# A hybrid decoder trunk: in the forgetting layer, three of four groups of probabilities are turned by VectorE and carried through DRAM

## The reference

```python
h = rmsnorm(x, g[0]); y = mixer(h); x = x + rmsnorm(y, g[1])
h = rmsnorm(x, g[2]); y = (silu(h @ Wg) * (h @ Wu)) @ Wd; x = x + rmsnorm(y, g[3])
```

```python
q, k, v, f_logit = split(h @ w_in)            # 32 heads of 64
c = cumsum(log_sigmoid(f_logit + b_f))        # per head, over tokens
s = q k^T / 8 + c_q - c_k, causal
p = softmax(s); out = (p v) @ w_out
```

## Time and profile before

| what | value |
|---|---|
| median of 3 runs | 2127.06 us (2127.04 to 2127.35) |
| profiled execution, its own time | 2127.44 us |
| its span in the trace | 2125.5 us |
| PE busy | 2115.1 us (100%), 9795 instructions |
| DVE (VectorE) busy | 1587.3 us (75%) |
| ACT (ScalarE) busy | 1180.5 us (56%) |
| POOL busy | 121.0 us (6%) |
| HBM traffic | 188 GB/s over the span |

### The profile page before, as it was taken

The page is one execution under the profiler, slowest core; times in us unless marked ns, Lnnn a source line. Parts: engine busy times, 40 slices in busy tenths (PEclk is TensorE's granted clock), DMA queues, the critical chain, the costliest instruction groups (busy, mean ns, idle before and its releaser), DMA issues.

```text
span 2125.5 us, 32513 instructions
## 1 busy us (share of the span) xinstructions
PE 2115.1 (100%) x9795; PEld 1735.5 (82%) x9795; DVE 1587.3 (75%) x3257; ACT 1180.5 (56%) x2133; POOL 121.0 (6%) x231
## 2 busy tenths in 40 slices
PE   9999999999999999999999999999999999999998
PEld 7877888888888888888878877888888888888886
DVE  6777577877668876678787777577776778776786
ACT  7776565544555444555676566565454555445453
POOL 2111000000000000000231131000000000000000
PEclk9999999999999999999999999999999999999999
DMA  7544856555666655665665664666655665556652
GB/s 259 189 139 133 215 180 219 187 188 177 203 211 190 195 172 193 197 206 156 185 197 182 181 195 160 207 199 198 198 174 182 197 216 187 187 179 198 216 186 91
DMA packets 205692, 399.85 MB, mean 188 GB/s; under 512 B 13248, under 2 KB 13664, under 8 KB 205104
## 3 DMA queue, kind: packets, MB, share of 16 engines
q1 hardware_dynamic: 203008, 389.86, 58.6%
q0 software_dynamic: 2320, 8.72, 1.4%
q10 hardware_dynamic: 288, 0.33, 0.0%
HBM read 396.72 MB, written 2.13 MB: 188 GB/s over the span
## 4 chain that ended last, share of the span: by engine, by line
PE 98%; DVE 1%; issue 1%; DMA 0%; POOL 0%; ACT 0%; SPq 0%; POOLq 0%; DVEq 0%; ACTq 0%
PE bank L1233 31%; PE bank L1235 31%; PE bank L1234 31%; PE bank L1282 1%; PE bank L1309 1%; PE bank L1293 1%; PE bank L1246 1%; DMA x_sb<-x 0%; PE bank L1265 0%; DVE ring_lo L759 0%; DVE x_sb L802 0%; DVE y_sb L1027 0%; POOL post_r L1126 0%; DVE a_lo L766 0%; DVE y_sb L795 0%
## 5 line engine op out<-in xcount | busy, mean ns | idle before, releaser
L1233 PE MATMUL bank<-ring_hi,a_hi 128*128 128x512 f32 x2240 | 884.0, 395 | 0.6 <-DVE ring_lo L759 0.6
L1235 PE MATMUL bank<-ring_hi,a_lo 128*128 128x512 f32 x2240 | 873.2, 390 | 0.0
L1234 PE MATMUL bank<-ring_lo,a_hi 128*128 128x512 f32 x2240 | 872.1, 389 | 0.0
L557 ACT ACTIVATE ring_hi<-stage,g_t 128x512 fp32r<-128x512 f32 x992 | 663.2, 717 | 340.1 <-DMA stage<-ffn_w_gate_up 202.4
L759 DVE SCALAR_TENSOR_TENSOR ring_lo<-stage,g_t,ring_hi 128x512 fp32r<-128x512 f32 x992 | 708.8, 760 | 162.1 <-ACT ring_hi L557 160.1
L1235 PEld LDWEIGHTS bank<-ring_hi,a_lo 128*128 128x128 f32 x2240 | 420.4, 188 | 88.8
L1233 PEld LDWEIGHTS bank<-ring_hi,a_hi 128*128 128x128 f32 x2240 | 420.6, 188 | 88.2 <-issue 4.1
L1234 PEld LDWEIGHTS bank<-ring_lo,a_hi 128*128 128x128 f32 x2240 | 421.0, 188 | 83.4
L757 DVE TENSOR_TENSOR ring_lo<-stage,ring_hi 128x512 fp32r<-128x512 f32 x480 | 306.7, 690 | 131.5 <-ACT ring_hi L555 130.2
L555 ACT ACTIVATE ring_hi<-stage 128x512 fp32r<-128x512 f32 x480 | 277.3, 624 | 167.7 <-PE bank L1235 150.0
L1233 PE MATMUL bank<-ring_hi,h_hi 128*128 128x512 f32 x704 | 274.4, 390 | 0.0
(11 more groups left out here) (144 smaller groups left out, 855.8 us busy)
## 6 DMA issues: line engine op xcount, KB each, us to landing
stage<-ffn_w_gate_up SPq DMA_DIRECT2D x352, 512.0 KB, 4.6
stage<-ffn_w_down SPq DMA_DIRECT2D x176, 512.0 KB, 5.6
stage<-fox_w_in SPq DMA_DIRECT2D x96, 512.0 KB, 4.1
stage<-swa_w_in SPq DMA_DIRECT2D x48, 512.0 KB, 4.5
stage<-swa_w_out SPq DMA_DIRECT2D x64, 256.0 KB, 4.1
stage<-fox_w_out SPq DMA_DIRECT2D x32, 512.0 KB, 4.6
g_b<-norm_gains POOLq DMA_DIRECT2D x4, 1024.0 KB, 5.9
cum_b<-cum_scratch POOLq DMA_DIRECT2D x32, 128.0 KB, 3.4
```

The costliest lines, as they stand in the source:

```text
L557: nc.scalar.activation(ring_hi[:, n % RING, :], src, ACT.Identity, scale=g_t[:, row * KT + j:row * KT + j + 1]).then_inc(hi_ready, 1)
L1233: nc.tensor.matmul(dst, hi_a, hi_w, start=start, stop=False)
L1234: nc.tensor.matmul(dst, hi_a, lo_w, start=False, stop=False)
L1235: return nc.tensor.matmul(dst, lo_a, hi_w, start=False, stop=stop)
```

## The change

It touches only the forgetting layer. The order of its units becomes keys, queries, values. A group's attention starts in its own value unit and goes on through the next two units, by a new table `FOX`; the last group has the table `FOX_LAST`. In the first three groups, P is no longer transposed by PE and copied by ScalarE. After each `normalise` (a pair of heads), VectorE turns the pair in 32x32 blocks inside each set of 32 partitions into `p_blocks` (one buffer). ScalarE stores `p_blocks` to DRAM in one DMA and, later, loads the blocks to their partitions in four DMAs of 32 partitions each into `p_f` (two buffers). `times_v` reads P from `p_f` with runs of 32 columns, one pair of heads at a time. The last group is turned on PE as before. Keys are turned in the query unit. POOL's bias loop is written out, and its buffers come free with the turned P. The steps of the forget gate and of the output's first heads are moved.

```diff
+FOX = dict(scores={6: (0, 1), 26: (2, 3)},
+           maxima={6: (0, 1), 12: (2, 3), 26: (4, 5), 32: (6, 7)},
+           exps={7: 0, 8: 1, 13: 2, 14: 3, 27: 4, 28: 5, 33: 6, 34: 7},
+           scaled={11: 0, 17: 1, 31: 2, 37: 3}, turned={},
+           pv={41: (0,), 52: (1,), 61: (2,), 72: (3,)}, out={53: 0, 73: 1},
+           stored={18: 0, 29: 1, 38: 2, 49: 3}, loaded={28: 0, 38: 1, 48: 2, 59: 3})
+FOX_LAST = dict(scores={6: (0, 1), 26: (2, 3)},
+                maxima={6: (0, 1), 8: (2, 3), 26: (4, 5), 28: (6, 7)},
...
+                pv={35: (0, 1), 52: (2, 3)}, out={})
-FG_STEPS = dict(split=34, gate=42, copy=44, turn=46, z=48, exp=50, log=52, cumulate=56, read=57)
+FG_STEPS = dict(split=28, gate=36, copy=38, turn=40, z=42, exp=44, log=46, cumulate=50, read=51)
-KEYS_TURNED = {True: (26, 27, 28, 30), False: (3, 7, 11, 15)}
+KEYS_TURNED = (1, 4, 7, 10)
 QUERIES_TURNED = (18, 20)
+LATE_O_FOX = {0: [(0, 1)], 2: [(1, 1)], 4: [(2, 1)], 6: [(3, 1)], 8: [(4, 1)], 10: [(5, 0), (5, 1)],
+              14: [(6, 0), (6, 1)], 27: [(7, 0), (7, 1)]}
...
+        p_f = at("p_f", 38 * KB + 256, [P, 2, P // Q, 6, Q])
+        p_blocks = at("p_blocks", 12 * KB, [P, P // Q, 6 * Q])
...
-            if U_FOX + 3 <= u <= U_FOX_OUT and (u - U_FOX) % 3 == 0:
-                return NG + (u - U_FOX) // 3 - 1
+            if U_FOX <= u < U_FOX_OUT and (u - U_FOX) % 3 == 2:
+                return NG + (u - U_FOX) // 3
...
+            def store_probabilities(G, i, m):
+                act.wait_ge(p_turned, HP * (G - NG) + m + 1 + HP * i)
+                act.dma_start(p_dram[m], p_blocks[:, :, :].rearrange("p b r -> p (b r)")).then_inc(p_stored, 16)
+
+            def load_probabilities(G, i, m):
+                act.wait_ge(p_stored, 16 * (HP * (G - NG) + m + 1) + 16 * HP * i)
...
+                blocks = p_dram[m].rearrange("(a j) (b r) -> b j a r", a=P // Q, b=P // Q)
+                for b in range(P // Q):
+                    act.dma_start(p_f[Q * b:Q * (b + 1), m % 2, :, :, :].rearrange("p a n i -> p a (n i)"), blocks[b]).then_inc(p_loaded[m % 2], 16)
...
+            def turn_probabilities(G, i, m):
+                n = HP * (G - NG) + m
+                dve.wait_ge(normed, GH * G + 2 * m + 2 + GH * i)
+                if n > 0:
+                    dve.wait_ge(p_stored, 16 * n + 16 * HP * i)
+                pair = prob[:, 2 * m % 4:2 * m % 4 + 2, :]
+                nc.vector.transpose(p_blocks[:, :, 0:2 * Q].rearrange("p b (h i) -> p h b i", i=Q),
+                                    pair[:, :, columns(0)].rearrange("p h (b j) -> p h b j", j=Q))
+                nc.vector.transpose(p_blocks[:, :, 2 * Q:6 * Q].rearrange("p b (h t i) -> p h t b i", t=2, i=Q),
+                                    pair[:, :, columns(1)].rearrange("p h (t b j) -> p h t b j", t=2, j=Q)).then_inc(p_turned, 1)
...
+            def times_v(G, i, m):    # as it reads now, in part
+                if part == 0 and not turned_by_dma(G):
+                    pe.wait_ge(pt_read, p_number(G, 2 * m + a) + 1)
+                elif part == 0 and a == 0:
+                    pe.wait_ge(p_loaded[m % 2], 64 * (2 * (G - NG) + m // 2 + 1) + 128 * i)
...
+                elif part == 0:
+                    p = p_f[:, m % 2, :, a:3 + 2 * a:2 + a, :].rearrange("p a t i -> p t a i")
+                else:
+                    p = p_f[:, m % 2, :, 3 + 2 * a, :]
```

More of the change, by code:

```diff
@@ L424, in qk_transposed @@
                 found.append((u, 0))
-            if holds_qk(u - 1) and s == 4 and not is_v(u):
+            if s == 4 and (holds_qk(u - 1) and not is_v(u) or u >= U_FOX and is_v(u)):
                 found.append((u - 1, 1))
@@ L662, in unit @@
                         if n in (0, 1):
-                            for kp, t in LATE_O.get(STEPS * n + s, ()):
+                            for kp, t in (LATE_O if u < U_FOX else LATE_O_FOX).get(STEPS * n + s, ()):
                                 o_heads(0 if u < U_FOX else 1, kp, t)
@@ L956, in unit @@
                         if n in (0, 1):
-                            for kp, t in LATE_O.get(STEPS * n + s, ()):
+                            for kp, t in (LATE_O if u < U_FOX else LATE_O_FOX).get(STEPS * n + s, ()):
                                 o_rests(0 if u < U_FOX else 1, kp, t)
                         if U_FOX <= u < U_FOX_OUT:
[L960 to L963, removed]
+                            part = (u - U_FOX) % 3
+                            if part == 1 and s in KEYS_TURNED:
+                                turn_keys(u - 1, i, KEYS_TURNED.index(s))
+                            if part == 1 and s in QUERIES_TURNED:
                                 turn_queries(u, i, QUERIES_TURNED.index(s))
@@ L1220, in _ @@
                     pool.wait_ge(y_gained, 16)
-                    with pool.Fori(0, NG) as c:
-                        for j in range(4):
-                            load_cum(0, c, j)
+                    for j in range(4):
+                        load_cum(0, j)
+                    for c in range(NG):
                         for j in range(GH):
-                            bias(0, c, j)
-                        pool.wait_ge(biased, GH * c + GH)
+                            bias(c, j)
         @block.tensor
@@ L1297, in times_v @@
                 n = GH * G + 2 * m
+                if m == 0 and G >= NG:
+                    pe.wait_ge(proj_read, 2 * mixer_unit(qk_unit(G) + 1) + 2 + 6 * i)
                 if m == 2 and (G + 1) % NG == 0:
```

88 lines of the change are left out of this document (58 added, 30 removed).

## The result

The changed kernel took 2153.82 us (median of four runs, 2150.63 to 2157.15) beside 2127.2 us for the kernel before on the same chip: 1.0126 times as long, 95% interval 1.0113 to 1.0138. That is 26.6 us slower, 23 us above the forecast and 15 us beyond the top of the range. The profiled execution took 2152.49 us, its span 2150.7, mean granted clock 0.994.

What follows compares the result with a forecast made beforehand. TensorE was taken to bound the kernel, its time the sum of its work. Work -6.4, waits +9.7 and gate +0.3 gave +3.6 us on the profiled execution's 2127.44, so a forecast median of 2130.7 us, range 2121 to 2139 for 8 in 10.

Steps and rivals of the forecast that it cites:

- the landing: P's transfers through DRAM: 3.5 us from a store's issue to landing (ends 2.8 and 4.1), 4.3 us for four loads.
- inside the ends: Extra traffic of 9.4 MB, 43 GB/s on 152 to 209: its share in a landing taken as within the landing's ends.
- The chain: DVE's turn waits for the last store; rests, maxima, exponentials and loads stand behind; PE waits 2.2 us at pair 1.
- the walk: DVE, ACT and PE programs laid side by side: 3.2 us of PE's waits a group, 9.7 us over three groups.
- The price hangs on the wait, not on the work: Single buffer `p_blocks`: PE's waits would be 0.2 us in all if it were always free in time, against 9.7 forecast.
- 0.2 in all with the buffer always free: PE's waits by the walk, were `p_blocks` always free in time: 0.2 us in all.
- the last rival: Weight path falls behind: `stage` freed late by idle DVE, SP's landings 4.1 to 5.5 us; 2135 to 2147 us, chance 0.12.
- the gate's chain: Forget gate's 12 steps from copy to sum now contain two key turns on DVE: 0 to 3.5 us, 0.3 taken.
- the query copy: DVE leaves the query unit full, so the copy of the queries ends 0.5 us late and the first scores wait that long.
- PE's work: 24 heads' transposes leave PE, -8.2 us; more interruptions by scores and PV add 1.8 us; together -6.4 us.
- The broken runs of 32 columns: PV reading P in runs of 32 columns: taken to cost nothing; at the other end each pair costs twice its 0.745 us.
- The two rules: Skill's rules: TensorE for 128x128 transposes, so the change loses; DMA landing 2.9 us for 393 KB, about 1 us below before.

Runs made afterwards that it cites:

- the kernel without transfers: Changed kernel with P turned but nothing stored or loaded; TensorE waits for the turn only and PV reads a zeroed buffer: 2125.25 us, ratio 0.9991.
- the kernel with two buffers and late pairs: Changed kernel with two p_blocks, PV of pairs 0 and 1 at step 62, of 2 and 3 at 86, loads at 64 and 68: 2123.95 us.
- the late products: Changed kernel with PV of pairs 0 and 1 at step 62, of 2 and 3 at 86, one p_blocks: 2149.31 us, ratio 1.0104.
- the filler: Changed kernel with 128x128 identity matmuls, result unused, ahead of PV of pair 1 in three groups: 40 took 2159.51 us, 20 took 2152.41.

## Why the prediction was wrong

**The term that failed is the landing.** The step was "I take 3.5 us from a store's issue to its landing, with ends 2.8 and 4.1", and 4.3 us for the four loads of a pair. Measured are 5.8 us as the stores' median (4.16 to 8.87 in the chain), 6.92 us for a pair's last load (2.8 taken), and 8.4 us from the first load's issue at 1173.53 to the product at 1181.90. The ends came from one store at the end of the run and from the weights' own loads, and neither row has another queue full beside it: here a store stands behind four loads of 96 KB, and the DMAs' share is 0.71 to 0.78 in the windows where it is on the way. The prediction counted the extra bytes (43 GB/s) and put their price "inside the ends". It was outside: even the weights went from 4.1 to 4.9 us. What of a landing is the weights' traffic and what the queue wasn't separated: the order in the queue decided which transfer was late, the size of the pieces hardly mattered, and no run took the weights away.

**The chain itself was right.** The wait stood where forecast: at PV, in pair 1, released by the load, behind VectorE's idle before the turns. Its size was 3.7, 3.8 and 5.1 us, not 2.2, and VectorE's idle sat in front of the third turn (4.3, 4.2 and 5.0 us, where the walk had 1.7) and not of the second (1.1, 0.6 and 0.8, where it had 3.0). "The price hangs on the wait, not on the work" holds: two buffers alone took 18.4 us away. But the sentence before it, 0.2 in all with the buffer always free, was too low for these steps of the table: 10.1 us over the kernel without transfers remained, and PV had to go later as well to lose it. A buffer that chains DMAs multiplies the error of one landing: it enters three times before pair 1's product (4.16 + 6.76 + 6.92 = 17.8 us, where I had 3.5 + 3.5 + 2.8 = 9.8), and the slack of the walk took up only part.

**By term:** the transfers cost 28.6 us by the medians where the sum had 9.7 for the waits, 18.9 more; the order cost 4.4 against 0.3, 4.1 more; the work on TensorE came out at the forecast 6.4. Together that is the 23 us by which the time lies above the forecast. By groups it is the same: 249.3 us over three, and 224.3 without transfers (77.2, 73.5, 73.5), so 8.4 us a group, not 3.2. The form that I took for the last rival, the weight path, was a small part: 1.1 us of waits at the products for `ring_lo`.

**The lower clock had no term.** It was granted for 6.83 us in each group after TensorE's wait, and TensorE was busy some 3 us longer for it: ten steps of a long matmul at 0.43 and not 0.23 us, the product itself 1.55 and not 0.87. With the wait filled most of that did not come back, since the pairs behind wait for the transfers anyway. In a kernel whose next works are not so bound it would be added.

**The order was under-costed:** 4.4 us against 0.3. The cause is in two places that the prediction had named at 0 to 3.5 us (the gate's chain) and at 0.5 us (the query copy). The second unit meets the one and the first value unit the other; there, a load of weights issued at 1051.15 took 7.88 us to land, beside the loads of the cumulated sums.

**What held.** PE's work: -6.4 forecast, -5.7 by the groups' lengths and -6.4 by the medians; a lone PV pair costs 1.01 us as an interruption (1167.77 to 1169.23 without transfers, less 0.45) where the terms give 0.945. The broken runs of 32 columns cost nothing: two pairs take the same time from `prob_t` before and from `p_f` in the kernel with two buffers and late pairs.

```profile
1181.28 1.52 PE L1309 MATMUL bank<-prob_t,v_sb 128*64 128x256 f32 x16
1190.96 1.52 PE L1387 MATMUL bank<-p_f,v_sb 128*64 128x256 f32 x16
```

Turning a pair: forecast 1.17 us, by groups of form (count, busy, mean ns, idle):

```profile
L893 DVE STREAM_TRANSPOSE p_blocks<-prob 128x512 f32<-128x512 f32 x12 | 8.0, 670 | 0.0
L891 DVE STREAM_TRANSPOSE p_blocks<-prob 128x256 f32<-128x256 f32 x12 | 5.3, 446 | 19.1 <-DMA p_scratch<-p_blocks 18.8
```

0.67 + 0.45 = 1.12 us: 128 partitions take as long as 32, so here the elements a partition set the time. Issues held ScalarE 0.35 us for a store and 0.46 for a load (0.4 and 0.5 forecast). One reading was misnamed without harm: the 0.45 us of the earlier trace rows end at the next L1234, not at the second.

**The two rules.** Turning P off TensorE lost here, and by 28.6 us of transfer against 5.7 us of gain; with two buffers and late products the same turns win 3.4 us over the kernel before. The Trainium skill, "VectorE: DVE Perf Modes", section "Rules for kernel authors", prefers TensorE for a 128x128 transpose; the first trace agrees with it and the best one (2123.95 against 2127.39) doesn't, so the schedule decided, not the operation. A store issued alone took 4.2 us to land beside the weights. By the Trainium skill, "DMA: Bandwidth & Descriptors", section "Anatomy of one DMA — SWDGE (gpsimd) path", the estimate for 393 KB had been 2.9 us; that section is on DMAs issued by GpSimd, and these were issued by ScalarE. The measurement decides, and it is twice that in the median (5.8). Nor did "about 1 us below the time before" follow: the prediction's own walk, with stores of 3.1 us, gives 3.7 us of waits, and so a time 2.4 us below.

## What to carry to other kernels

- Price a DMA that a wait hangs on by rows of a stretch as loaded as its own, and widen the range for what stands ahead of it in its queue; where no such row exists, the upper end isn't the dearest row of a quiet one.
- A single buffer between a compute engine and a DMA puts every landing in series on an in-order engine; a second buffer, or an issue right behind the write, took away 18 to 21 of 29 us. With one buffer moving the consumer later won 4.5 us, with two 11.4.
- If a wait disappears and the time doesn't, look for who is still idle: the late products had no wait left, and VectorE's 23 us of idle came out at a copy.

## What was not expected of the hardware

- In ScalarE's queue a pair 0's store, issued alone, let VectorE go after 4.61, 4.16 and 4.39 us; a pair 1's, issued behind four loads of 96 KB, after 6.86, 6.76 and 7.57.
- Putting the stores first made the loads late instead: their median landing went from 5.7 to 6.6 us, the longest from 8.3 to 10.6.
- Four times as many pieces (768 instead of 3072 bytes) cost 0.3 us in the loads' landing (5.7 against 5.4).
- A matmul of 128x128 in the filler left two records, one started every 0.11 us: 20 of them took 4.62 us, and 40 took 9.1 where 4.5 had been expected.
- After waits of 3.7 to 5.1 us at pair 1 TensorE was granted 0.50 of its clock for 6.83 us, three times of three; with 20 matmuls in the wait's place, never. The length of a wait alone doesn't tell: behind the first scores' wait the clock fell after 1.9 us in the changed kernel and after 2.1 without transfers, and stayed full after 2.8 with the 20 matmuls and after 2.9 with two buffers and late pairs.
